# A recurrent chunk whose steps stand at other products of its loop body, with heads scaled by ScalarE and transposed by TensorE

## What is computed

```python
s = jnp.einsum('bhtd,bhsd->bhts', qc, kc) * Dm
num = w_int[..., None] * jnp.einsum('bhvd,bhtd->bhtv', C, qc) + jnp.einsum('bhts,bhsv->bhtv', s, vc)
den = w_int * jnp.einsum('bhd,bhtd->bht', n, qc) + jnp.sum(s, axis=-1)
h = num / jnp.maximum(jnp.abs(den), jnp.exp(-m_t))[..., None]
C_new = f_end[..., None, None] * C + jnp.einsum('bhs,bhsv,bhsd->bhvd', w_end, vc, kc)
...
h = h * lax.rsqrt(jnp.mean(h * h, axis=-1, keepdims=True) + EPS)
h = (h.reshape(B, L, D_M) * head_norm_w.astype(f32)).astype(x.dtype)
h = h * jax.nn.sigmoid(o_pre) * jax.nn.silu(z_m)
```

## Time and profile before

| | us |
|---|---|
| median of 3 runs | 2467.45 (2467.15 to 2469.88) |
| the profiled execution, its own time | 2466.87 |
| its span, first to last instruction | 2465.1 |
| PE busy, share of the span | 2361.0 (96%) |
| DVE busy | 1501.0 (61%) |
| ACT busy | 933.5 (38%) |
| POOL busy | 95.1 (4%) |

### The profile page before, as it was taken

The page is one execution under the profiler, slowest core; times in us unless marked ns, Lnnn a source line. Parts: engine busy times, 40 slices in busy tenths (PEclk is TensorE's granted clock), DMA queues, the critical chain, the costliest instruction groups (busy, mean ns, idle before and its releaser), DMA issues. The chain is left out here.

```text
span 2465.1 us, 41811 instructions
## 1 busy us (share of the span) xinstructions
PE 2361.0 (96%) x14825; PEld 2281.4 (93%) x14825; DVE 1501.0 (61%) x2680; ACT 933.5 (38%) x1701; POOL 95.1 (4%) x82
## 2 busy tenths in 40 slices
PE   7998999999999999999989999999998999999998
PEld 7997999899999999999989999999998999998886
DVE  4334778799876876777557787777654533333333
ACT  4333444344454444444445444444453210011211
POOL 0003000000110000000011000000000000000000
PEclk9998999999999999999999999999998999999999
DMA  6443655455766664565756665565575733344442
GB/s 207 133 131 118 182 195 177 140 181 179 228 224 208 210 202 142 175 182 167 244 161 197 203 221 167 162 191 164 172 211 164 242 118 98 98 131 145 140 141 87
DMA packets 425376, 421.41 MB, mean 171 GB/s; under 512 B 31546, under 2 KB 365498, under 8 KB 425270
## 3 DMA queue, kind: packets, MB, share of 16 engines
q1 hardware_dynamic: 425270, 420.01, 54.5%
HBM read 293.13 MB, written 126.85 MB: 170 GB/s over the span
## 5 line engine op out<-in xcount | busy, mean ns | idle before, releaser
L1485 PE MATMUL b_g<-x_hi,w_hi 128*128 128x344 f32 (+1 forms) x3024 | 989.2, 327 | 28.7 <-DVEq L1107 9.1
L1485 PE MATMUL b_g<-x_lo,w_hi 128*128 128x344 f32 (+1 forms) x3024 | 969.4, 321 | 0.0
L1485 PE MATMUL b_g<-x_hi,w_lo 128*128 128x344 f32 (+1 forms) x3024 | 967.2, 320 | 0.0
L1485 PEld LDWEIGHTS b_g<-x_hi,w_hi 128*128 128x128 f32 x3024 | 571.5, 189 | 38.6 <-issue 10.3
L1485 PEld LDWEIGHTS b_g<-x_lo,w_hi 128*128 128x128 f32 x3024 | 571.8, 189 | 1.7
L1485 PEld LDWEIGHTS b_g<-x_hi,w_lo 128*128 128x128 f32 x3024 | 571.8, 189 | 0.0
L990 ACT ACTIVATE w_hi<-w_operands 128x512 fp32r<-128x512 f32 x533 | 333.7, 628 | 390.0 <-PE b_g L1485 381.6
L1121 DVE TENSOR_TENSOR w_lo<-w_operands,w_hi 128x512 fp32r<-128x512 f32 x533 | 373.1, 711 | 1.8 <-ACT w_hi L990 1.0
L1816 PE MATMUL c_g<-act_hi,RH 128*128 128x294 f32 x896 | 268.8, 300 | 10.5 <-DVE act_lo L1766 10.5
L1816 PE MATMUL c_g<-act_hi,RL 128*128 128x294 f32 x896 | 268.7, 300 | 0.0
L1816 PE MATMUL c_g<-act_lo,RH 128*128 128x294 f32 x896 | 268.3, 299 | 0.0
(11 more groups left out here) (258 smaller groups left out, 2598.5 us busy)
## 6 DMA issues: line engine op xcount, KB each, us to landing
w_operands<-w_in SPq DMA_DIRECT2D x288, 256.0 KB, 5.2
w_operands<-w_ops_d SPq DMA_DIRECT2D x36, 768.0 KB, 4.8
stages<-w_ops_d SPq DMA_DIRECT2D x36, 768.0 KB, 4.9
stages<-w_in SPq DMA_DIRECT2D x72, 256.0 KB, 3.1
w_operands<-w_ops_d SPq DMA_DIRECT2D x72, 256.0 KB, 6.3
w_ops_d<-w_operands SPq DMA_DIRECT2D x18, 768.0 KB, 3.3
w_ops_d<-stages SPq DMA_DIRECT2D x18, 768.0 KB, 3.5
w_ops_d<-w_operands SPq DMA_DIRECT2D x36, 256.0 KB, 3.9
```

The source lines that it names most:

```text
L1485: last = nc.tensor.matmul(bank[:, 0:n], w[:, j, k, :], x[:, k, 0:n], start=(j < 4 and k == 0 and m == 0), stop=(k == 3 and m == 2), skip_g ...
```

## The change

The heads stand at places 4, 6, 8 and 9 on PE, DVE and ACT alike (`HEADS`). PE transposes k at place 1. DVE scales k at 2 instead of 1, multiplies scores by decay at 3 instead of 2, takes the mean square at 10 instead of 11, and multiplies into the gate after place 13's whole work (called 14, at the body's end) instead of ahead of it. The diagonals are gone: at 12 ACT scales the four heads' `h` in place, and at 13 PE transposes them.

```diff
+    HEADS = (4, 6, 8, 9)
...
     def chunk(c, at):   # ACT
-                elif at in (4, 6, 8, 10):
-                    h = (at - 4) // 2
+                elif at in HEADS:
+                    h = HEADS.index(at)
...
+                elif at == 12:
+                    act.wait_ge(rs_set, c + 1)
+                    for h in range(NH):
+                        last = nc.scalar.activation(HB[:, h, :], HB[:, h, :], ACT.Copy, scale=ss[:, 2, h:h + 1])
+                    last.then_inc(hn_set, 1)
...
     def chunk(c, at):   # DVE
                 if at == 0:
                     dve.wait_ge(m_in, 16 * (c + 1))
-                    dve.wait_ge(ht_done, 1 + c)
...
-                elif at == 1:
+                elif at == 2:
                     dve.wait_ge(kt_done, c + 1)
                     dve.wait_ge(cu_done, 1 + NH * c)
                     nc.vector.tensor_tensor(KW[:, :, :], PT[0][:, :, :], bc(tk["w_end"][:, bass.ds(NH * c, NH)], P),
                                             ALU.mult).then_inc(kw_set, 1)
-                elif at == 2:
                     dve.wait_ge(kq_in, 32 * (c + 1))
...
                     nc.vector.tensor_tensor(QW[:, :, :], QW[:, :, :], qT[:, :, :], ALU.mult).then_inc(qw_set, 1)
+                elif at == 3:
                     dve.wait_ge(s_done, c + 1)
...
-                elif at in (3, 5, 7, 9):
+                elif at in HEADS:
...
-                elif at == 11:
+                elif at == 10:
                     dve.wait_ge(sq_set, 1 + NH * (c + 1))
...
-                elif at == 12:
-                    dve.wait_ge(rs_set, c + 1)
-                    for h in range(NH):
-                        last = nc.vector.tensor_scalar(Dm[:, h, :], g.ident[:, :], ss[:, 2, h:h + 1], None, ALU.mult)
-                    last.then_inc(hn_set, 1)
-                elif at == 13:
+                elif at == 14:
                     dve.wait_ge(ht_done, 1 + c + 1)
                     dve.wait_ge(gate_in, 16 * (c + 1))
...
     def body(p, s, i, extra, before):   # DVE
+                if extra == "chunk":
+                    chunk(chunk_of(p, s, i), 14)
...
     def chunk(c, at):   # PE
+                elif at == 1:
                     pe.wait_ge(hg_set, 1 + c)
                     for h in range(NH):
                         last = nc.tensor.transpose(PT[0][:, h, :], kT[:, h, :], g.ident[:, :])
                     last.then_inc(kt_done, 1)
-                elif at in (3, 5, 7, 9):
+                elif at in HEADS:
...
                 elif at == 13:
                     pe.wait_ge(hn_set, c + 1)
                     for k in range(KB):
-                        last = nc.tensor.matmul(PT[k // 4][:, k % 4, :], HB[:, k // 2, (k % 2) * P:(k % 2 + 1) * P], Dm[:, k // 2, :],
-                                                start=True, stop=True)
+                        last = nc.tensor.transpose(PT[k // 4][:, k % 4, :], HB[:, k // 2, (k % 2) * P:(k % 2 + 1) * P], g.ident[:, :])
                     last.then_inc(ht_done, 1)
```

More of the change, by code:

```diff
@@ L1241, in chunk @@
                     nc.vector.tensor_tensor(PT_[:, :, :], PS[:, :, :], Dm[:, :, :], ALU.mult).then_inc(p_set, 1)
-                elif at in (3, 5, 7, 9):
-                    h = (at - 3) // 2
+                elif at in HEADS:
+                    h = HEADS.index(at)
                     ch = bass.ds(NH * c + h, 1)
```

## The result

| | before | after |
|---|---|---|
| median, us | 2467.30 of 4 runs (2466.13 to 2469.88) | 2488.18 of 4 runs (2484.34 to 2493.98) |
| the profiled execution | 2466.87 | 2484.34, the fastest of its four |
| its mean TensorE clock | 0.988 | 0.983 |

The changed kernel takes 1.0088 times as long, with a 95% interval of 1.0075 to 1.0100: slower by 20.9 us. The other three runs of the change have spans of 2492.2, 2485.1 and 2487.8 us at mean clocks of 0.980, 0.981 and 0.979, all lower than 0.983, so the profiled one shows less of what the clock costs than most. A mean clock tells how long a run stood at half clock (twice its shortfall from 1, times the span): 85 us in the profiled run, and by the rounded means some 94 to 105 in the others.

A forecast was written before the change was run, and what follows sets the result against it. PE bounds the kernel, busy 2361.0 of 2465.1 us. From 2466.9: -13.8 transposes, +7.9 chunk ends, -8.2 chunk 6, -2.9 heads, +18.5 scores gives 2468.4; +24 clock gives 2492 us, range 2462 to 2504.

The forecast's parts named there:

- The scores: PE's wait for the scores: DVE's longer chain makes lateness 3.4 instead of 1.88 in eight chunks; +18.5 us over all chunks.
- upper bound of +22: Upper bound of the +18.5 us at the scores, if each wait in a loop cost 0.1 us more.
- Transposes: Chunk's end on PE: eight transposes replace diagonal products, saving 0.92 us in each of 15 chunks; -13.8 us.
- The end of a chunk: PE's wait ahead of the transposes: ACT's four scalings end later than DVE's diagonals did; +7.9 us.
- Chunk 6: Diagonals on DVE no longer collide with POOL's sums; PE's long idle and the half-clock stretch behind it go; -8.2 us.
- Heads: Heads 2 and 3 at later places: PE's six waits of 0.3 us for ACT's `h` go; -2.9 us.
- Without the clock: Whole kernel, all terms but the clock's: 2468.4 us, no change, the longer stall eating the cheaper transposes.
- The clock: Behind the scores' stalls: TensorE falls to half clock in eight of twelve long stalls, 3.0 us each; +24 us.
- Rival 1: The clock falls in only three to five chunks; +12 us, 2480 us; chance 0.20.
- Rival 2: The clock never falls, idle at the scores staying under 1.9 us if faster; 2468 or 2460 us; chance 0.26.
- Rival 3: The clock also falls at chunk ends, transposes behind a 0.8 us stall counting as idle; up to 2540 us; chance 0.04.
- Rival 4: At the scores the change does not do what it says, since DVE catches up elsewhere; excluded, given no chance.

The follow-up runs named there:

- filled kernel: The whole change plus seven useless 128x128 matmuls ahead of PE's wait for the scores in every chunk; 2465.77 us, ratio 0.9992 to the kernel before.
- second experiment: Also `e_tr`: the kernel before, in its old order, with only ACT's scaling of the heads and PE's transposes; 2457.16 us, ratio 0.9956.
- e_kw1: The whole change, but DVE scales k at place 1 again, the scores staying at 3; 2463.18 us, ratio 0.9976 to the kernel before.
- e_order: The change's moved steps alone, with the old diagonals on DVE and diagonal products on PE; 2490.91 us, ratio 1.0087 to the kernel before.
- experiments 6 and 7: 6: the change with k's scaling at 1, scores at 2, gate products at 13; 2425.06 us. 7: also ACT's scaling at 11; 2408.37 us.

## Why the prediction was right

The forecast was 2492 (2485 to 2504 in its own case, 2462 to 2504 in all), the median 2488.18. It was right by the mechanism that it put ahead of the others, and its steps show as they were worked out, but for the price of one fall. That eight fell in the profiled run is partly luck: the forecast chose eight out of twelve long stalls by judgement, and nothing in its rows gave that number.

- **The scores.** The sum had an idle of 3.2 in the loops, 2.4 in chunks 0 and 7 (a lateness of 2.6 less 0.16), 2.8 in chunks 4 and 13, and 1.4 in the last `gates` chunks. Measured were 3.12, 2.36, 2.84 and 1.37. The waits were put near 43 and are 40.8. The chain on DVE could be added up from the rows of before, since its order is fixed and each duration was to be had there. The row-wide product with the wait for its own end was put at 1.0 and took 0.91. The upper bound of +22 follows from 0.1 per wait only with some four waits in each loop chunk, which the sum doesn't list; nothing hangs on it.
- **Transposes.** Eight take 0.85 us; the sum had 0.8 to 0.9.
- **The end of a chunk.** The wait was put near 0.8 in sixteen and is 0.86. ACT's four scalings took 1.69 us, where the sum had 1.57 from a row of another instruction. An estimate by the Trainium skill (ScalarE: Activation LUTs, What ACT_TABLE_LOAD costs) had 0.49 for one, which with starts 0.40 apart gives the 1.69; the trace agrees with it, and the wait was 0.06 longer than worked out.
- **Chunk 6.** The sum had -8.2. The 5.7 and the fall behind it are gone, and the whole stretch from chunk 6 to 7 is 9.4 shorter. POOL does hold DVE's `w_lo` there, as said, and PE waits 0.88 at that place like elsewhere:

```profile
1269.19 3.12 POOL L930 TENSOR_TENSOR x_quarters<-x_quarters 128x1360 f32<-128x1360 f32 x1
...
1269.37 7.00 DVE L1127 TENSOR_TENSOR w_lo<-w_operands,w_hi 128x512 fp32r<-128x512 f32 x2
...
1273.33 1.09 PE L1546 MATMUL b_t<-ident,h 128*128 128x128 f32 x8 [0.88 <-ACT h L1064]
```

- **Heads.** PE's six waits for `h` are gone from the profile, as the -2.9 had it.
- **Without the clock** the sum gave 2468.4. A body without a fall is 1.0 longer, which is what -0.92, +0.42 and +1.5 give. The filled kernel, which has no fall in any chunk, measures 2465.8: 2.6 below, of which its shorter bodies are about 1.5.
- **The clock: the term that was mis-sized.** The number of falls was forecast as eight, and eight fell. The price of one was put at 3.0, from a stretch of 6.8 us in the earlier trace rows. Five of the eight lasted 3.4 us and cost 1.3 to 1.6, three lasted 6.8 and cost 2.7 to 2.8; the mean is 2.0, and the term is 16 where the sum has 24. The step that failed is the one from a single stretch of the trace to all of them. The profiled run is the fastest of four, however, and between the medians the clock takes some 21 us. By their mean clocks the slower runs stood at half clock for 9 to 19 us more. How many falls that is, and whether all lie in the chunks, can't be seen, so that the median came so close to 2492 is in part luck too.
- **The rivals.** Rival 1 (three to five falls) is excluded by the count of eight. Rival 2 (no falls, 2468 or less) is what the filled kernel shows: its time is right for a kernel that keeps the clock, and the change isn't one. Its bound of 1.9 us is not borne out as one above which the clock falls: two stalls of 2.25 and six of 2.54 were not followed by a fall (table below). Rival 3 (falls at the chunk's end, since transposes behind a stall would count as idle) is excluded: all 16 such places in the second experiment kept the clock at 1.00. The Trainium skill (TensorE: Matmul & The Clock Gate, Part 4: PE-mode transpose) says that a transpose doesn't count as PE-busy the same way; no run here shows an effect of that for eight transposes behind a stall of 1 us. Rival 4, that DVE would catch up elsewhere, did not come.

**What stays open.** These are all stalls at the scores of over 1.7 us in the profiled executions, and how many had a half-clock stretch that began between 1.2 us before PE's restart and 1.4 behind it:

| idle at the scores, us | kernel | stalls | with a fall |
|---|---|---|---|
| 1.72 | before; `e_tr` | 10; 10 | 0; 0 |
| 1.76, 2.25, 2.54 | `e_kw1` | 2, 2, 8 | 0, 0, 2 |
| 2.36 | the change; `e_order` | 2; 2 | 2; 2 |
| 2.85 | the change; `e_order` | 2; 2 | 1; 0 |
| 3.12 | the change; `e_order` | 8; 8 | 5; 6 |

So the length of a stall does not decide alone. All four of 2.36 us were followed by a fall, and six of eight of 2.54 were not; chunks 1, 3 and 8 of the change kept the clock behind 3.12. What tells them apart isn't settled. The lengths of the falls show a pattern: the four of 6.8 us at the scores (three in the change, one in `e_order`) began 0.9 to 1.2 us before PE was back at work, the others 0.5 us before at most, or behind it. Neither was tried in a run of its own. Nor could the falls of the runs without a profile be counted.

## What to carry to other kernels

When a step is moved within in-order queues, count each instruction that now stands between its release and the one that another engine waits for: here 2.6 us of row and 0.7 us of delay, read off the profile of before, gave PE's stall to 0.1 us. Then hold the stall's length against the stalls at which the clock has fallen in the same trace; the 0.6 us more per chunk between the fourth kernel and the change cost more by the clock (about 13 us in the profiled runs) than by the waiting (9.4), though the length of a stall alone does not foretell a fall. And give a consumer more time (the head at 4 instead of 3) only with its inputs left where they were; putting k and the scores back turned a loss of 20.9 us into a gain of 34.5, and two more steps on DVE and ACT (experiments 6 and 7) made it 59.9.

## What the runs showed of the hardware

- **A fall can come after the stall is over.** PE's timeline at chunk 9 of the change:

```profile
1611.20 0.67 PE L1540 MATMUL b_s<-v_ones,k_weighted 128*128 128x257 f32 x2 [3.12 <-DVE scores L1246]
...
1612.14 1.06 PE L1542 MATMUL b_n<-C_state,q_weighted 128*128 128x257 f32 x2
```

  PE was back at work at 1611.20, and the half-clock stretch shown above begins at 1612.14, 0.9 us later. So all of its 3.40 us lay on work. At phase B's end it fell within the idle time; a search for falls must look behind a stall as well as in it. The latest began 1.4 us behind PE's restart (chunk 1 of `e_kw1`: restart at 1057.95, clock down from 1059.37). In chunk 10 of the change it fell first, at 1649.68, 1.2 us before PE was back:

```profile
1650.86 1.20 PE L1540 MATMUL b_s<-v_ones,k_weighted 128*128 128x257 f32 x2 [3.11 <-DVE scores L1246]
```

- **The half-clock stretches had two lengths**, about 3.4 us and about 6.8, where the trace of before showed one in this part of the program.
- **The same program stretch can stand at another clock in another kernel.** The clock came back some 7 us earlier at the start of phase B with the same instructions there, and fell once more behind it, and that moved 2.1 us into the span. Whether two runs of one kernel differ in this way isn't shown.
- **ACT's scaling of 128x256 with a scale from a tile** started every 0.40 us, against 0.37 taken from `h` with the same shape.
